# Moving the norm's root behind the first product of the mixers in a hybrid decoder trunk

## The reference

```python
def _rmsnorm(x, g):
    y = x * lax.rsqrt(jnp.mean(x * x, axis=-1, keepdims=True) + EPS)
    return y * g
# a layer
x = x + 0.5 * _rmsnorm(_swiglu(_rmsnorm(x, ng[0]), w_up, w_down), ng[1])
h = _rmsnorm(x, ng[2])            # the mixer's entry norm
h = mixer(h)                      # begins with proj = h @ w_in
x = x + _rmsnorm(h, ng[3])
x = x + 0.5 * _rmsnorm(_swiglu(_rmsnorm(x, ng[4]), w_up, w_down), ng[5])
```

## Time and profile before

| | |
|---|---|
| median of the runs | 2759.89 us |
| profiled execution, span from first to last instruction | 2756.7 us |
| TensorE busy | 2666.6 us (97%) |
| VectorE busy | 1528.1 us (55%) |
| ScalarE busy | 1158.3 us (42%) |
| GpSimd busy | 283.6 us (10%) |
| mean granted TensorE clock | 0.987 of full |
| chain that ended last | TensorE 83%, VectorE 9%, ScalarE 4%, GpSimd 2%, issue 2%, DMA 1% |

### The profile page before, as it was taken

The page is one execution under the profiler, slowest core; times in us unless marked ns, Lnnn a source line. Parts: engine busy times, 40 slices in busy tenths (PEclk is TensorE's granted clock), DMA queues, the critical chain, the costliest instruction groups (busy, mean ns, idle before and its releaser), DMA issues.

```text
span 2756.7 us, 52164 instructions
## 1 busy us (share of the span) xinstructions
PE 2666.6 (97%) x22237; PEld 2515.3 (91%) x22237; DVE 1528.1 (55%) x1842; ACT 1158.3 (42%) x1571; POOL 283.6 (10%) x294
## 2 busy tenths in 40 slices
PE   7999999999999999999999999999999999989998
PEld 7998987999999886699999989799999989978998
DVE  4556744655565445465465553565555558446554
ACT  4434544543444344343344333343343335435442
POOL 0000004100200125110010000010010000042000
PEclk9999999999999999999999999999999999999999
DMA  5544532554544535444455453454455455135443
GB/s 190 167 138 146 158 89 65 168 168 139 178 157 145 189 112 168 137 153 161 142 171 167 141 175 121 130 173 163 149 169 167 140 153 153 57 101 163 158 141 101
DMA packets 415628, 404.26 MB, mean 147 GB/s; under 512 B 14787, under 2 KB 411951, under 8 KB 415087
## 3 DMA queue, kind: packets, MB, share of 16 engines
q1 hardware_dynamic: 411348, 397.42, 45.5%
q0 software_dynamic: 4096, 4.20, 0.6%
HBM read 385.19 MB, written 16.39 MB: 146 GB/s over the span
## 4 chain that ended last, share of the span: by engine, by line
PE 83%; DVE 9%; ACT 4%; POOL 2%; issue 2%; DMA 1%; SPq 0%; POOLq 0%; ACTq 0%
PE psum L363 21%; PE psum L364 20%; PE psum L365 20%; DVE w_lo L345 2%; DVE x L576 1%; DVE y L574 1%; POOL fbuf L424 1%; ACT w_hi L338 1%; PE psum L2730 1%; DVE g_cacc L1624 1%; POOL fbuf L420 1%; PE psum L1164 1%; PE psum L1049 1%; PE psum L1181 1%; PE psum L2116 1%
## 5 line engine op out<-in xcount | busy, mean ns | idle before, releaser
L345 DVE TENSOR_TENSOR w_lo<-raw,w_hi 128x2048 fp32r<-128x2048 f32 (+3 forms) x366 | 747.0, 2041 | 525.3 <-ACT w_hi L338 525.2
L363 PE MATMUL psum<-xn_hi,w_hi 128*128 128x288 f32 x3248 | 970.0, 299 | 10.2 <-DVE w_lo L345 6.8
L364 PE MATMUL psum<-xn_lo,w_hi 128*128 128x288 f32 x3248 | 961.1, 296 | 0.0
L365 PE MATMUL psum<-xn_hi,w_lo 128*128 128x288 f32 x3248 | 957.9, 295 | 0.0
L338 ACT ACTIVATE w_hi<-raw 128x2048 fp32r<-128x2048 f32 (+3 forms) x366 | 623.7, 1704 | 714.4 <-PE psum L365 672.4
L363 PEld LDWEIGHTS psum<-xn_hi,w_hi 128*128 128x128 f32 x3248 | 611.6, 188 | 19.5 <-issue 8.6
L365 PEld LDWEIGHTS psum<-xn_hi,w_lo 128*128 128x128 f32 x3248 | 614.5, 189 | 0.0
L364 PEld LDWEIGHTS psum<-xn_lo,w_hi 128*128 128x128 f32 x3248 | 613.0, 189 | 0.6
L364 PE MATMUL psum<-h_lo,w_hi 128*128 128x288 f32 x1408 | 415.5, 295 | 0.0
L363 PE MATMUL psum<-h_hi,w_hi 128*128 128x288 f32 x1408 | 415.0, 295 | 0.0
L365 PE MATMUL psum<-h_hi,w_lo 128*128 128x288 f32 x1408 | 414.9, 295 | 0.0
(11 more groups left out here) (578 smaller groups left out, 3129.8 us busy)
## 6 DMA issues: line engine op xcount, KB each, us to landing
raw<-w_ffn_up SPq DMA_DIRECT2D x176, 1024.0 KB, 5.1
raw<-w_ffn_down SPq DMA_DIRECT2D x64, 768.0 KB, 4.2
raw<-w_ffn_down SPq DMA_DIRECT2D x64, 640.0 KB, 3.9
raw<-gdn_w_in SPq DMA_DIRECT2D x32, 1024.0 KB, 5.9
raw<-mlstm_w_in SPq DMA_DIRECT2D x12, 1024.0 KB, 5.4
raw<-gdn_w_out SPq DMA_DIRECT2D x8, 1024.0 KB, 6.7
raw<-cache_mla_latent SPq DMA_DIRECT2D x64, 128.0 KB, 2.2
a_split<-cache_mla_latent SPq DMA_DIRECT2D x64, 128.0 KB, 2.3
```

The costliest lines, as they stand in the source:

```text
L345: dve.tensor_tensor(spread(w_lo[slot(u, i)], u), packed(raw[u % NRAW], u), spread(w_hi[slot(u, i)], u).bitcast(F32), ALU.subtract).then_in ...
L363: pe.matmul(out, wh[:, k, c], hi(k), start=st, stop=False)
L364: pe.matmul(out, wh[:, k, c], lo(k), start=False, stop=False)
L365: last = pe.matmul(out, wl[:, k, c], hi(k), start=False, stop=sp_)
```

## The change

All four mixers are entered in the manner of the FFNs: tile by tile, from `g * x` without the root. The root is multiplied in afterwards.

```diff
-        def act_pre(act, n):            # and dve_pre, pe_sum_squares, the
-            ...                         # fillers after the sums: gone
+        def act_enter(act, n):          # was act_pre_ffn, now for all
             ...
+            if subs[n][0] == "ffn":
+                act_split(act, ubase[n] + 2)
+                act_square_x(act, n, H - 1)
+            else:
+                act_square_x(act, n, H - 1)
+                act_split(act, ubase[n] + 2)

+        def pe_enter(pe, n, outs):
+            u0 = ubase[n]
+            pe.wait_ge(lo_ready, u0 + 1)
+            pe.wait_ge(second_lo_ready, n + 1)
+            weights = [tuple(entry_weights(n, g)) for g in range(2)]
+            for k in range(KC):
+                pe.wait_ge(xhi_ready, entered(n) + k + 1)
+                for g, out, c in outs:
+                    hi, lo = weights[g]
+                    pe.matmul(out, hi[:, k, c], xn_hi[:, k, :], ...)
+                    pe.matmul(out, lo[:, k, c], xn_hi[:, k, :], ...)
+                pe.wait_ge(xlo_ready, entered(n) + k + 1)
+                for i, (g, out, c) in enumerate(outs):
+                    last = pe.matmul(out, weights[g][0][:, k, c], xn_lo[:, k, :], ...)
+                    ...
```

GDN: GpSimd multiplies the root into `cbuf` between ScalarE's copy and the convolution, then into the tails and z:

```diff
         def pool_gdn(pool, n):
+            pool.wait_ge(r_ready, 2 * n + 1)
+            once(pool, "g_cbuf_set", 1)
+            for i in range(12):
+                once(pool, "g_evac", i + 1)
+                v = cbuf[:, i % 2, :, 3:3 + SEQ]
+                pool.tensor_tensor(v, v, rp.to_broadcast([P, 2, SEQ]), ALU.mult)
+                v = by_token(cbuf[:, i % 2, :, 3 + SEQ:CW])[:, :, :, 3:7]
+                pool.tensor_tensor(v, v, rs..., ALU.mult).then_inc(sem("g_cbuf_normed"), 1)
+            ...                         # tail: two multiplications
+            for j in range(4):
+                ...                     # z: 128x576 each
         def pe_gdn(pe, n):
+            pe_enter(pe, n, [(0, psum[:, m, 0:T], tile(m)) for m in range(2)] + [(1, psum[0:32 + HG, 4, 0:T], ...)])
             ...                         # histories turned
+                if i > 0:
+                    pe_unit(..., ready=(lambda k: pe_enter_sums(pe, n) if k == 6 else None) if i == 1 else None)
         def act_gdn(act, n):
             for i in range(12):
-                act_split(act, u0 + i + 2)
-                if i < 2:
-                    act_gates(act, i)
+                if i not in (0, 2):
+                    act_split(act, u0 + i + 2)
+                if i == 1:
+                    act_root(act, 2 * n)
+                    act_gates(act, 0)
+                    act_split(act, u0 + 4)
         def dve_gdn(dve, n):
+            dve_split(dve, u0 + 2)
             ...
+            dve_split(dve, u0 + 3)
+            dve.wait_ge(unit_used, u0 + 2)
+            dve.wait_ge(r_ready, 2 * n + 1)
+            ...                         # gate rows times root, one op more
-            once(dve, "g_evac", i + 1)
+            once(dve, "g_cbuf_normed", i + 1)
```

MLA: the latents' norms hold for any factor, so only their epsilon is weighted: EPS times the sum of squares is added by one fp32 matmul to each of the two sums; the rotary key gets one multiplication more. The entry sums are done ahead of the first of them:

```diff
+                    once(pe, "a_craw", 2)
+                    pe_enter_sums(pe, n)
+                    pe.matmul(psum[:, 4, 0:T], at_("norm")[:, 0:1].to_broadcast([P, P]), sq_total, ...)
```

More of the change, by code:

```diff
@@ L282, in trunk @@
         NSUB = len(subs)
-        entries = [u for u, sub in zip(ubase, subs) if sub[0] == "ffn"]
+        entries = list(ubase)
         def slot(u, i=0):
@@ L401, in trunk @@
         squares_before = lambda q: H * q + q // 2
[L403 to L409, removed]
         sq_sum, sum_step = sem("sq_sum"), sem("sum_step")
         sq_part, sq_total = fbuf[:, 0], fbuf[:, 1, 0, :]
-        summed = lambda q: q // 2 + 1 + sum(s_[0] == "ffn" for s_ in subs[:(q + 1) // 2])
-        steps_before = lambda q: 2 * (q // 2) + 3 * sum(s_[0] == "ffn" for s_ in subs[:(q + 1) // 2])
+        steps_before = lambda q: 5 * (q // 2) + 3 * (q % 2)
         def pool_sums(pool, q):
@@ L513, in dve_enter @@
                     chunk(i)
-                if i > 0 and ffn:
+                if i > 0 and n < NSUB:
                     dve_low_x(dve, n, i - 1)
[L517 to L537, removed]
@@ L622, in pair @@
                         pe_enter_sums(pe, n)
[L624 to L633, removed]
[L634 to L642 removed]
+            pe_enter(pe, n, [(g, psum[:, 4 + 2 * g + m, 0:T], tile(m)) for g in range(2) for m in range(2)])
             pair(1, 0, 1)
@@ L915, in pe_gdn @@
             gi, u0 = subs[n][2], ubase[n]
[L916 to L926 removed]
+            pe_enter(pe, n, [(0, psum[:, m, 0:T], tile(m)) for m in range(2)] + [(1, psum[0:32 + HG, 4, 0:T], slice(0, 32 + HG))])
             once(pe, "g_conv_in", 16)
@@ L2015, in pe_mlstm, with ml_columns @@
             pe_out(pe, n, u0 + 13, xn(xn_hi), xn(xn_lo), None, first=1)
-        def ml_columns(pe):
+        def ml_columns(pe, n):
             once(pe, "l_pre_rows", 1)
+            pe.wait_ge(r_ready, 2 * n + 1)
+            for p in range(2):
+                pe.matmul(psum[:, 7, 155 + p:156 + p], rr[0:1, 0, tile(p)], ones[0:1, 0:1], start=True, stop=True)
+            for h in range(LH):
+                pe.matmul(psum[quarter(h), 7, 157:158], smp(rr[0:1, 0, :]), ones[0:1, 0:1], start=True, stop=True)
             for r, row in enumerate((LA, LWJ, LNT)):
@@ L2560, in pe_mla @@
             u0 = ubase[n]
-            ready = x_chunks(pe, n)
-            for i in range(2):
-                pe_unit(pe, u0 + i, [psum[:, 2 * i, 0:T], psum[:, 2 * i + 1, 0:T]], xn(xn_hi), xn(xn_lo),
-                        True, True, ready=ready if i == 0 else None)
+            pe_enter(pe, n, [(g, psum[:, 2 * g + m, 0:T], tile(m)) for g in range(2) for m in range(2)])
             u = u0 + 2
```

305 lines of the change are left out of this document (155 added, 150 removed).

## The result

The changed kernel took 2769.1 us (2763.6 to 2773.2, 6 runs) against 2760.5 for the kernel before beside it: ratio 1.0032, 95% interval 1.0020 to 1.0044. It is slower by 8.6 us, where I forecast 2758.2 and no change that can be told.

The account below looks back on a forecast made before the run. TensorE, busy 97% of the span, was taken as the bound; only its waits or useless products could be had. -4.8 - 10.9 + 12.0 + 2.0 = -1.7 against 2756.7 gives 2755.0, plus 3.2 is 2758.2 us; 8-in-10 range 2740 to 2777.

Parts of the forecast that it names:

- Clock: GDN, idle stretch of about 10 us ahead of a product: lower granted clock costs 1.0 us each, +2.0 in all (0 to +4).
- mLSTM: mLSTM's entry: products 2 and 3 follow product 1 without a gap, gate columns start earlier; -4.8 us (-7.8 to -2.5).
- Common part: GDN and mLSTM entries: entry product ends at t = 11.3, product 1 runs 16.2 to 24.7, root there at 22.1.
- MLA: MLA's entry: both first products end at t = 14.5 instead of 26.9; -10.9 us in sum (-12 to -9).
- GDN, product 4: Each GDN: VectorE's chain from the root makes product 4 start at t = 48.0 instead of 45.5; +2.5 us (-0.2 to +4.4).
- The two rounds behind it: Each GDN, product 4 to 7: GpSimd's 1.75 us makes two rounds 15.45 instead of 13.7; +1.7 us.
- The squares' rounds: GDN rounds while squares are summed: a round takes 7.7 us anyhow, so 0.
- Gate columns: Each GDN, gate columns: wait for VectorE's copies and take GpSimd's step in full; +1.75 us.
- GDN as a whole: Both GDN sub-layers: +6.0 us each, +12.0 together, with 1.0 of clock for each counted separately.
- Median against the span: Whole kernel: the median of the runs lies 3.2 us above the profiled span, turning 2755.0 into 2758.2 us.
- Rival A: GDN: the lead of product 1 holds, keeping 6 us in each; -27.7 us in all, 2732; chance 0.17.
- Rival B: GDN: GpSimd's multiplication sticks behind splits, 1.85 us more a round, 15 in each GDN; +16 us, 2776; chance 0.23.

## Why the prediction was wrong

The failed step is the term "Clock", +2.0 in all, "between 0 and +4": the mechanism was named, its extent was mis-sized. Filling the idle stretches took 14 to 16 us off the changed kernel. I had counted one stretch in each GDN and 1.0 us for each. The runs show:

- In each GDN there are several: product 1 behind its wait for the split, product 4 (2.3 and 1.3 us), product 6 (1.5 in both), and the gate columns in part. Waits of 2.1 and 2.5 us, which I had priced at their length, were followed by falls too. Together 5.7 and 6.6 us at product 11, 1.3 and 2.2 of it by the end of product 1.
- In mLSTM I put none. My own working ends the entry product at 11.3 and starts product 1 at 16.2, and I did not look at the clock behind that gap (3.9 us of it were idle). With the idle filled the sub-layer is 6.1 us shorter than before, against -4.8 forecast; without, 0.5. So the lead that the term describes is there, inside its range, and 5.6 us of clock in the profiles ate it (the two kernels with GDN as before differ by 5.6 by their medians and 3.6 by their ratios).

Without the clock term my sum is -4.8 - 10.9 + 12.0 = -3.7. The kernel with all idle stretches filled, which is the change without that term, stands 5.2 under the kernel before beside it. The other steps, in order, of which some came right by luck:

- *Common part*: product 1 from 16.05 to 24.50 (16.2 to 24.7), the root at 21.6 (22.1). The numbers are right, in part by luck. I had TensorE wait from 18.6 to 20.2 for a sum held back by the second split. In the run the small casts stood first, the split began at t = 18.1 behind the adds, and nothing waited for the sum; the lower clock kept product 1 back instead. With the idle filled it takes 7.1 us instead of 8.5, and the root is used at t = 20.4. The blocking itself is right: the rule of the Trainium skill that I used (SBUF — State Buffer, section Who interferes with whom) is borne out by these rows, and by those of the multiply-adds (3.84 against 3.06 us), of which I had no row.
- *MLA*: the entry products' copy at 973.54, t = 14.7 (14.5); -10.6 (-10.9). Right.
- *GDN, product 4* at 47.98 (48.0), the idle stretch 10.7 us (10.5). The chain from the root's first use was right, 26.3 us against 25.9. The start was right by luck, for the root itself came 1.3 us late by the clock: with all filled, product 4 starts at 46.6, 1.1 after the kernel before and not 2.5. In the second GDN it starts at 48.8, since product 1 fell to the lower clock for longer.
- *The two rounds behind it*: 17.45 instead of the forecast 15.45; 2.3 of clock, and a wait of 2.1 us where before had 0.66.
- *The squares' rounds*: 0, right, apart from product 6's clock. *Gate columns*: wait 1.88 instead of 0.2, so +1.7 (+1.75).
- *GDN as a whole*: the first sub-layer's +7.1 against 7.0 is luck. At product 11 it stands 10.7 us behind the kernel before; the work behind that took 170.1 us in this execution and 173.7 in that of before. The second, 10.8 behind at product 11, ends at +10.1. With all filled, product 11 is 5.0 and 4.2 us behind, against the 6.0 of my terms without the clock.
- *Median against the span*: I carried 3.2 us from before to after. The profiled execution of after was its fastest; the median lay 5.5 above its time and 7.4 above its span. Of the 10.9 us between 2758.2 and 2769.1, 4.2 are this; the other 6.7 are in the profile.

Rival A did not come: no lead got past the convolutions. Rival B came in part: its sign, a multiplication above 2.5 us, is there. GpSimd's multiplication took 2.1 to 2.95 us where a split ran beside it and 1.1 to 1.3 where none did, but that was three rounds of twelve. Its 15 us a GDN did not come. The step and what it drags along in the clock cost 7, the step alone 4.7 and 4.0 (product 11 of the two kernels with fillers, with and without it), near the 5.0 that my terms gave it (1.5, 1.7 and 1.75).

What stays open: why mLSTM's falls at t = 80 to 90 and 140 to 150 vanish once product 1 runs at full clock, and also in both kernels with the other order of squares and split, where it doesn't. They come where TensorE is busy throughout, so idle time doesn't explain them; no run here separates the moment at which that work comes from what precedes it. So that fillers hold the clock is shown where they stand; that they also remove falls further on is seen, and not explained.

## What to carry to other kernels

Where a change opens an idle stretch of TensorE, read the granted clock in the windows behind it and price it with the wait: here 1.3 to 2.3 us at products 1, 4 and 6. Not every wait is followed by a fall (product 6 behind 2.1 us kept the full clock in the kernel with the other order of squares and split), so read it in more than one profile. Fill the stretch with matmuls that nobody reads, fewer than reach the end of the wait, for any filler past it is paid in full (2.7 us here), and place them behind no wait that is itself late. And apply an early entry mixer by mixer: where the root can be multiplied in without a step in the chain that ends last (MLA, mLSTM) it paid 10.6 us and, with fillers, 6.1; where it cost GpSimd a step in each round it lost.

## What the runs showed of the hardware

- *The lower clock meets a busy TensorE too.* In mLSTM of after TensorE is busy for 5.00 of 5 us and granted 0.75. In GDN the 25 us from t = 100 on are granted 0.73 to 0.86 in every kernel; in the kernel before TensorE is busy for all of them (25.00 us, clock 0.86 and 0.80).
- *Executions of one kernel differ by the clock.* The part of a GDN from product 11 to the leave root is the same work in all kernels and took 170.1 to 179.7 us in the profiles. Over the whole kernel, eight runs of one (GDN as before, mLSTM's order taken back) took 2746.7 to 2750.0 us at a mean clock of 0.986 and 2753.3 to 2757.1 at 0.983 to 0.984. That is how a gain seen up to product 11 can be smaller in the median, and why the two profiles understated the loss here. The two GDN of after from 125 us on (same columns as above):

```profile
364.70:524.88 160.18, 150.31 (x2375) 1.00 0.34 100
2366.38:2530.71 164.33, 157.51 (x2384) 0.96 0.33 97
```

- *The lock holds off small instructions too.* The cast of 128 columns at 255.60 took 1.40 us and ended with GpSimd's add; in the kernel before, with GpSimd idle, it took 0.23. The Trainium skill has this as well (same section: casts can take the shared port), and the row agrees.
- *The clock falls while TensorE idles and comes back under fillers.* The fall to 0.50 in the idle stretch and the return under fillers (0.69, then 1.00) fit the Trainium skill's sentence that "the default state is throttled, and activity releases the throttle" (TensorE: Matmul & The Clock Gate, section The HAM clock gate). The falls of a busy TensorE, the first point of this list, do not fit it by themselves.
